# Half tiles of w_out, two top-k blocks side by side, and an earlier S5 and GLU in a two-layer hybrid encoder on one core

## What is computed

```python
proj = h @ w_in
q, k, v, qi, ki, wi, u = jnp.split(proj, IN_SPLITS, axis=-1)
attn = dsa_attention(q, k, v, qi, ki, wi)      # 128 best keys of each query by an index score
y = s5_ssm(u, ...)                             # diagonal state space scan over 512 channels
y = jax.nn.gelu(y)
y = y * jax.nn.sigmoid(y @ glu_w + glu_b)
mixed = jnp.concatenate([rms_norm(attn, attn_gain), rms_norm(y, ssm_gain)], axis=-1)
return mixed @ w_out                           # (512, 1024) @ (1024, 1024)
```

## Time and profile before

| | |
|---|---|
| median of 3 runs | 2172.32 us (2168.12 to 2175.24) |
| time of the profiled execution | 2174.77 us |
| its span | 2172.8 us |
| PE busy, share of the span | 2066.5 us, 95% |
| DVE busy | 1347.1 us, 62% |
| ACT busy | 706.7 us, 33% |
| mean granted clock of TensorE | 0.951 |

### The profile page before, as it was taken

How to read it: one execution, slowest core, us unless ns; L and a number is a source line. 1 busy time by engine, 2 the same in 40 slices (tenths; PEclk the granted TensorE clock), 3 DMA queues, 4 the chain that set the end, 5 groups by cost and what they waited for, 6 DMA issues and landing times.

```text
span 2172.8 us, 25378 instructions
## 1 busy us (share of the span) xinstructions
PE 2066.5 (95%) x9564; PEld 1666.1 (77%) x9564; DVE 1347.1 (62%) x2099; ACT 706.7 (33%) x1066; POOL 243.1 (11%) x219
## 2 busy tenths in 40 slices
PE   6999899999689999999999999999978999999998
PEld 5788778877467788888888877888755678888887
DVE  5768846567884664543467787466688646555334
ACT  3332222342434432222342322234234433222123
POOL 0006900300000000000000294040000000000000
PEclk8999999999669999999999999999986799999999
DMA  7475556342110263533347364553330024454332
GB/s 261 126 214 179 161 147 179 97 113 69 49 39 11 87 202 118 187 97 104 88 125 223 119 196 131 156 146 101 88 88 20 20 59 158 143 165 128 114 90 75
DMA packets 395985, 264.77 MB, mean 122 GB/s; under 512 B 56560, under 2 KB 371672, under 8 KB 395864
## 3 DMA queue, kind: packets, MB, share of 16 engines
q1 hardware_dynamic: 386784, 259.89, 40.1%
q10 hardware_dynamic: 9080, 3.26, 0.7%
HBM read 254.98 MB, written 6.29 MB: 120 GB/s over the span
## 4 chain that ended last, share of the span: by engine, by line
PE 76%; DVE 14%; issue 5%; ACT 3%; DMA 1%; ACTq 0%; SPq 0%; DVEq 0%; POOL 0%; POOLq 0%
PE ps L1650 22%; PE ps L1651 22%; PE ps L1652 22%; DVE w_lo L990 3%; DVE mod_acc L1011 2%; DVE score L1367 2%; DVE small L1365 2%; PE ps L1910 1%; PE ps L1929 1%; ACT w_hi L684 1%; PE ps L1937 1%; PE ps L1920 1%; DVE x L1096 1%; DMA stage<-in_ffn_w 1%; PE ps L1858 1%
## 5 line engine op out<-in xcount | busy, mean ns | idle before, releaser
L1650 PE MATMUL ps<-h_hi,w_hi 128*128 128x512 f32 x1728 | 687.4, 398 | 17.7 <-DVE w_lo L990 13.8
L1651 PE MATMUL ps<-h_lo,w_hi 128*128 128x512 f32 x1728 | 679.4, 393 | 0.0
L1652 PE MATMUL ps<-h_hi,w_lo 128*128 128x512 f32 x1728 | 679.1, 393 | 0.0
L990 DVE TENSOR_TENSOR w_lo<-stage,w_hi 128x1024 fp32r<-128x1024 f32 (+2 forms) x322 | 394.4, 1248 | 103.2 <-ACT w_hi L684 99.3
L1650 PEld LDWEIGHTS ps<-h_hi,w_hi 128*128 128x128 f32 x1728 | 327.5, 190 | 99.0 <-issue 16.4
L1652 PEld LDWEIGHTS ps<-h_hi,w_lo 128*128 128x128 f32 x1728 | 328.1, 190 | 70.0
L1651 PEld LDWEIGHTS ps<-h_lo,w_hi 128*128 128x128 f32 x1728 | 328.0, 190 | 65.7 <-issue 0.5
L684 ACT ACTIVATE w_hi<-stage 128x1024 fp32r<-128x1024 f32 (+2 forms) x322 | 318.7, 1016 | 173.1 <-PE ps L1652 164.9
L1650 PE MATMUL ps<-g_hi,w_hi 128*128 128x512 f32 x704 | 276.4, 393 | 2.4 <-DVE g_lo L1303 2.4
L1651 PE MATMUL ps<-g_lo,w_hi 128*128 128x512 f32 x704 | 274.2, 389 | 0.0
L1652 PE MATMUL ps<-g_hi,w_lo 128*128 128x512 f32 x704 | 274.1, 389 | 0.0
(11 more groups left out here) (300 smaller groups left out, 1859.1 us busy)
## 6 DMA issues: line engine op xcount, KB each, us to landing
stage<-in_ffn_w SPq DMA_DIRECT2D x210, 512.0 KB, 4.6
mod_stage<-in_mod_w SPq DMA_DIRECT2D x144, 512.0 KB, 5.5
stage<-in_ffn_w SPq DMA_DIRECT2D x64, 448.0 KB, 4.0
stage<-in_w_in SPq DMA_DIRECT2D x20, 512.0 KB, 4.0
...
```

Of the source, the lines that this page charges most:

```text
L990: V.tensor_tensor(w_lo[:, c % RING, 0:n], stage[:, c % RING, 0:n], w_hi[:, c % RING, 0:n].bitcast(F32), ALU.subtract).then_inc(w_split_lo. ...
L1650: mm(out, hi, rhs_hi, start=first, stop=False)
L1651: mm(out, hi, rhs_lo, start=False, stop=False)
L1652: return mm(out, lo, rhs_hi, start=False, stop=last)
```

## The change

- w_out is loaded in half tiles. Chunks 16 to 19 of the mixer hold the y half for two output tiles each, chunks 20 to 23 the attention half. The bytes are the same.
- The y halves of output tiles 0 to 3 (y_half) run inside heads 19 to 22, and their part is added to x on its own in heads 20 to 23 (mix_update). Those tiles get a second update later, so four more DVE instructions stand in a layer. keep_streaming begins at head 24.
- Behind head 31 PE runs the y halves of tiles 4 to 7, then eight attention halves (att_half) on their own. Splits 20 and 21 move into heads 21 to 24, splits 22 and 23 ahead of the updates; two of the eight steps still have a split.
- Top-k: a round is topk_max and topk_take, each waiting for its own block's last step (mark, need) and with its own eight values. Two blocks run side by side: 1 and 2 in heads 0 to 7, 2 and 3 in heads 8 to 15, 3 alone in heads 16 to 23, one round a block and head. Eight rounds of block 1 run before head 0, four of them between the index scores.
- S5: states after tiles 4, 5, 6 and 8, outputs after 5, 6, 7 and 9, with three buffers u8 in place of two, and SP's stores and fetches for them move with it. All four GELUs are computed ahead of head 0. The GLU is one group of 12 matmuls in each of heads 4 to 7, and what follows it (norm, ssm_t, mix_done) ends in head 18, not 27.

```diff
 FFN_CHUNKS = 2 * FT + KT * NP
-X_STEPS = 2 * NP * KT + KT
-X_LAST = ((NP - 1) * KT, NP * KT, NP * KT + KT + (NP - 1) * KT)
+EARLY_OUT = 4
+MIX_STEPS = EARLY_OUT + KT
+X_STEPS = 2 * NP * KT + MIX_STEPS
+X_LAST = ((NP - 1) * KT, NP * KT + EARLY_OUT, NP * KT + MIX_STEPS + (NP - 1) * KT)
...
-STATES_AT = {5: 0, 6: 1, 9: 2, 10: 3}
-Y_AT = {7: 0, 8: 1, 10: 2, 11: 3}
+STATES_AT = {4: 0, 5: 1, 6: 2, 8: 3}
+Y_AT = {5: 0, 6: 1, 7: 2, 9: 3}
...
-GLU_AT = {8 + 2 * n + j: (n, j) for n in range(ST) for j in range(2)}
...
+GLU_AT = {4 + n: n for n in range(ST)}
...
+HALF_AT = {19 + n: n for n in range(EARLY_OUT)}
+HALF_X_AT = {20 + n: n for n in range(EARLY_OUT)}
...
-KEEP_FROM = 22
...
-OUT_SPLIT_AT = {10: 16, 12: 17, 15: 18, 17: 19}
+KEEP_FROM = 24
+TOPK_WITH = [(1, 2)] * HEADS + [(2, 3)] * HEADS + [(3,)] * HEADS + [()] * HEADS
...
+    def mark(self, i):
+
+        i.then_inc(self.sem, 1)
+        self.n += 1
+        return self.base + self.n
+
+    def need(self, value):
+
+        self.eng.wait_ge(self.sem, value)
+
...
+                if m < 20:
+                    return tiles(a["w_out"], layer, AT, ST, (m - 16) * 2 * P, 2 * P)
+                return tiles(a["w_out"], layer, 0, AT, (m - 20) * 2 * P, 2 * P)
 
...
-                            if m == 9:
-                                u_store(l, 0)
-                                u_store(l, 1)
-                                u_fetch(l, 0)
-                                u_fetch(l, 1)
-                            if m == 10:
-                                u_store(l, 2)
-                                u_store(l, 3)
-                            if m in (14, 15):
-                                y_store(l, m - 14)
-                                u_fetch(l, m - 12)
-                                y_fetch(l, m - 14)
-                            if m in (17, 18):
-                                y_store(l, m - 15)
-                                y_fetch(l, m - 15)
+                            if 8 <= m < 12:
+                                u_store(l, m - 8)
+                            if 9 <= m < 12:
+                                u_fetch(l, m - 9)
+                            if m in (12, 13, 14, 16):
+                                y = min(m - 12, ST - 1)
...
-                    step(V.memset(score[b][0:64, (b + 1) * P - 64:(b + 1) * P], INADM))
-
-                def topk_round(b):
-
-                    s = score[b]
+                    dve.wait_ge(*idx_acc.at(l, b * IDX_HEADS - 1))
+                    topk_last[b] = step.mark(V.memset(score[b][0:64, (b + 1) * P - 64:(b + 1) * P], INADM))
+
+                def topk_max(b):
+
+                    step.need(topk_last[b])
                     settle(dve)
-                    step(V.max(top8[:], s))
+                    topk_last[b] = step.mark(V.max(top8[b % 2], score[b]))
+
+                def topk_take(b):
+
+                    step.need(topk_last[b])
                     settle(dve)
-                    step(V.match_replace(out=s, in_to_replace=top8[:], in_values=s, imm_value=TAKEN))
+                    topk_last[b] = step.mark(V.match_replace(out=score[b], in_to_replace=top8[b % 2], in_values=score[b], imm_value=TAKEN))
...
 
+                def mix_update(n, bank, even, c):
+
+                    if n % 2:
+                        used(dve, l, c)
+                    else:
+                        dve.wait_ge(*even.at(l, n // 2))
+                    V.scalar_tensor_tensor(out=x[:, n, :], in0=ps[:, bank, :], scalar=gate[:, 1, n:n + 1],
+                                           in1=x[:, n, :], op0=ALU.mult, op1=ALU.add).then_inc(x_new.sem, 1)
+
...
+                                (topk_max, topk_take)[n % 2](1)
                         topk_start(t - INDEX_FROM + 1)
-                    for _ in range(TOPK_EARLY.get(t, 0)):
...
                     mask_head(e)
+                    if len(blocks) > 1:
+                        topk_max(blocks[1])
+                    if blocks:
+                        topk_take(blocks[0])
                     if b:
                         att_step(b - 1, h)
                     if b > 1 and h == 0:
                         att_step(b - 2, 8)
-                    for _ in range(TOPK_AT.get(e, 0)):
-                        topk_round(TOPK_BLOCK[rounds])
-                        rounds += 1
-                        if rounds == len(TOPK_BLOCK) or TOPK_BLOCK[rounds] != TOPK_BLOCK[rounds - 1]:
-                            topk_end(TOPK_BLOCK[rounds - 1])
+                    if len(blocks) > 1:
+                        topk_take(blocks[1])
...
+                    if e in HALF_X_AT:
+                        n = HALF_X_AT[e]
+                        mix_update(n, 4 + n % 2, half_even, m0 + 16 + n // 2)
...
+                split_lo(l, m0 + 23)
                 for n in range(KT):
-                    if n < KT - 2:
-                        split_lo(l, m0 + 20 + n)
+                    if n in (2, 4):
+                        split_lo(l, m0 + 23 + n // 2)
                     if n:
                         add_squares(l, KT + n - 1)
-                    update(l, 1, n, m0 + 16 + n)
+                    if n >= EARLY_OUT:
+                        mix_update(n, OUT_BANK[n - EARLY_OUT], out_even, m0 + 20 + n // 2)
+                    else:
+                        if n >= 2:
+                            dve.wait_ge(*x_new.at(l, NP * KT + n))
+                        mix_update(n, n % 2, out_even, m0 + 20 + n // 2)
                     scaled_lo(l, 2, n)
...
+                    c = m0 + 16 + n // 2
+                    if n % 2 == 0:
+                        chunk_ready(l, c)
+                    if 2 <= n < 6:
+                        pe.wait_ge(*x_new.at(l, NP * KT + n - 2))
+                    bank = 4 + n % 2 if n < EARLY_OUT else OUT_BANK[n - EARLY_OUT]
+                    for k in range(ST):
+                        if n == 0:
+                            pe.wait_ge(*mix_done.at(l, k))
+                        i = split3(ps[:, bank, :], half_tile(c, k, n % 2), h_hi[:, AT + k, :], h_lo[:, AT + k, :],
+                                   k == 0, n < EARLY_OUT and k == ST - 1)
+                    if n % 2:
                         i.then_inc(w_used.sem, 1)
-
-                def out_half(n, first, last):
-
-                    c = m0 + 16 + n
-                    if first == AT:
+                    elif n < EARLY_OUT:
+                        i.then_inc(half_even.sem, 1)
+
+                def att_half(n):
+
+                    c = m0 + 20 + n // 2
+                    if n % 2 == 0:
                         chunk_ready(l, c)
-                        if n >= 4:
-                            pe.wait_ge(*x_new.at(l, NP * KT + n - 4))
-                    for k in range(first, last):
-                        if n == 0 and k >= AT:
-                            pe.wait_ge(*mix_done.at(l, k - AT))
-                        i = split3(ps[:, OUT_BANK[n % 4], :], w_tile(c, k), h_hi[:, k, :], h_lo[:, k, :], k == AT, k == AT - 1)
-                    if first == 0:
-                        i.then_inc(w_used.sem, 1)
+                    if n in (2, 3):
+                        pe.wait_ge(*x_new.at(l, NP * KT + EARLY_OUT + n - 2))
+                    bank = n % 2 if n < EARLY_OUT else OUT_BANK[n - EARLY_OUT]
+                    for k in range(AT):
+                        i = split3(ps[:, bank, :], half_tile(c, k, n % 2), h_hi[:, k, :], h_lo[:, k, :],
+                                   n < EARLY_OUT and k == 0, k == AT - 1)
+                    i.then_inc((out_even, w_used)[n % 2].sem, 1)
 
...
                     if e in GLU_AT:
-                        glu(*GLU_AT[e])
+                        glu(GLU_AT[e])
+                    if e in HALF_AT:
+                        y_half(HALF_AT[e])
```

More of the change, by code:

```diff
@@ L239, in trunk @@
         small = sb("small", [P, SMALL])
-        ms, rstd, mhalf, cols, top8, rinv, nmax, ones = (small[:, i:i + n] for i, n in (
+        ms, rstd, mhalf, cols, top8a, rinv, nmax, ones = (small[:, i:i + n] for i, n in (
             (0, 4), (4, 4), (8, 4), (12, 4), (16, 8), (24, HEADS), (32, 2), (34, 1)))
+        top8 = (top8a, small[:, 64:72])
         half_bias, half_gain, bias_col = small[:, 54:58], small[:, 58:62], small[:, 62:64]
@@ L922, in mixer_act @@
                 act.wait_ge(*h_done.at(l, 2 * KT - 1))
-                for m in range(2):
-                    act.wait_ge(*y_in[m].at(l, 16 * 2 * GI - 1))
-                    gelu(m)
+                gelu(3)
+                for m in range(ST):
+                    gelu_high(m)
                 for e in range(NA):
@@ L1439, in s5_scan @@
                     half = (slice(0, NS), slice(NS, P))
-                    step(*(V.tensor_tensor(hs[half[g], 0, :, g, 1:J + 1], X[0][half[g]], M[0][half[g]], ALU.subtract) for g in range(2)),
-                         V.tensor_tensor(hs[half[0], 1, :, 0, 1:J + 1], X[1][half[0]], M[1][half[0]], ALU.add))
+                    step.need(re)
```

(17 more changed lines are left out.)

157 lines of the change are left out of this document (92 added, 65 removed).

## The result

The changed kernel takes 2147.19 us (2145.30 to 2147.57), the kernel before, timed beside it, 2171.28. The ratio is 0.9886 [0.9868, 0.9904]: faster by 1.1%, with 2148 forecast. The spans of the two profiled executions differ by 27.0 us.

The account below looks back on a forecast made before the run. PE is busy for 95% of the span, so only waits and slow stretches could go. Terms of -14.3 us (layer 0) and -13.0 (layer 1) from 2174.8 gave 2147.5, so 2148; own range 2138 to 2160, with rivals to 2168.

Parts of the forecast that it names:

- a place that I had set at 0: Start of the next FFN after the mixer: low clock in both kernels, so counted 0, at worst +2 us.
- Ahead of head 0: Before the first logits: scans +0.8 us net, PE's idle wait 4.1 in place of 5.87; sum -1.0 a layer.
- Block 0: Heads 0 to 7: shorter top-k, added GLU, clock rising after 6.4 us; mask 8 at +24.6, sum -0.3 us.
- Block 1: Heads 8 to 15: top-k without gaps and PE work give 31.0 us; -4.4, in layer 1 -3.1.
- the bunching: Block 1: PE's work of about 28 us is bunched in head 13, so 1.5 us was added.
- Block 2: Heads 16 to 23: y_half(0) starts at +11.5, then heads take 2.7 + 1.9 us; mask 24 at +33.5, sum -1.0.
- Block 3: From mask 24 to the last values: PE's head unchanged, one keep_streaming group gone; -0.8 us.
- w_out: End of the mixer: first update 14.1 us behind the last values, not 16.7; steps 25.6, not 29.8; sum -6.8.
- gaps that stay: Rival, top-k rounds: the 0.15 us is a cost of each top-k instruction, not of waiting; 2166 us, chance 0.13.
- a clock that stays low in heads 4 to 7 and 19 to 22: Rival: clock stays at 1.2 GHz through the GLU and y halves; +9 us a layer, 2193 us, chance 0.06.
- costly scans: Rival, early S5: PE's waits between projections bring the clock down; +5 us a layer, 2158 us, chance 0.12.
- half a gain at the end: Rival, w_out: first update stays at 16.7 us and a step waits for ACT; -3, 2156 us, chance 0.08.

Follow-up runs that it names:

- the run with chained waits: The changed kernel, same instruction order, with each top-k step waiting for the last counted DVE step of whichever block, not its own block's: 2154.03 us, 0.9922.

## Why the prediction was right, point by point

- *The sum.* Forecast -14.3 and -13.0 a layer. To the next FFN's first product the trace has -12.9 in layer 0 and -11.3 in layer 1. Another 2.9 us were gained behind layer 1's mixer, a place that I had set at 0. In the kernel before, the first 12 us of the FFN behind the mixer were, in layer 0 (layer 1 has the same, at 0.60):

```profile
733.37:745.37 12.00, 12.00 (x46) 9.74 (x47) 3.68 (x5) 3.03 (x4) 1.98 (x1) 0.61 0.40 116
```

  After, the clock is 0.63 and 0.87 there. PE does wait 6.7 us ahead of both, as forecast (6.5); the low stretch just ends sooner once, and 60 matmuls go into the 12 us instead of 46. I would call that luck; no run isolates it. Without it the sum would have missed by 3 us, still inside the range.
- *Ahead of head 0.* Forecast 4.1 us of idle PE and -1.0; measured 3.45 and -0.7 (layer 1: 3.77). The -0.7 can't be told from nothing, since profiles of kernels that are alike up to there reach mask 0 up to 2.5 us apart; the wait can. A scan takes 6.5, not the 6.7 that I took. The early scans cost PE no more than 0.95 us of wait at one place.
- *Block 0.* 24.6 forecast, 24.75 and 25.9 measured. The clock rose 3.2 us after the first GLU matmul in layer 0 and only behind the twelfth, 5.3 us on, in layer 1; I had taken 6.4. So the block by itself is over a microsecond longer than I forecast, and in layer 0 an early rise hid that: the hit there is luck.
- *Block 1.* 31.0 forecast, 30.1 and 29.4 measured: the bunching that I added didn't cost 1.5. The mechanism was half of the story, though. I took the gap of 0.15 us for the whole gain; the run with chained waits gives it 2.7 and 3.3 us of block 1 in the two layers, of the 5.3 and 4.6 by which the block got shorter.
- *Block 2.* Forecast -1.0, measured -0.1 and, in layer 1, +0.8. This term was mis-sized: y_half(0) starts 13.1 us behind mask 16 and not 11.5, and a head with a y half takes 4.7 to 4.8, not 4.6.
- *Block 3.* -0.8 forecast, -0.4 measured in both layers by the same marks (27.39 and 27.00): the keep_streaming group was worth half of what I took.
- *w_out.* First update 14.2 us behind the last values (14.1 forecast); steps 2.73, 4.75, 3.33, 4.75, 3.33, 3.32, 3.33 (2.7, 4.75, 3.33, 4.75, three of 3.33). -6.2 in place of -6.8.

The rivals: gaps that stay, a clock that stays low in heads 4 to 7 and 19 to 22, costly scans and half a gain at the end are each refuted by the trace. The Trainium skill, "VectorE: DVE Perf Modes", section "The DRAIN you can't avoid", has it that a semaphore after each DVE instruction costs nothing over one at the end, by a measurement on copies. Here, for steps that wait for the one just ahead, it cost 0.15 us each, and 7 us in all. The price that I had put on the rival with the gaps was too high, though: with 64 of the 96 gaps ahead of a value load back, the run with chained waits lost 3.4 us a layer, where I had put 9.5 on all of them.

What the prediction did not see is that its own terms hide parts of very different worth. By the runs, from the kernel before on: top-k order -25 us beside its own runs of the kernel before (2146), early S5 and GELUs -7 (2139), early GLU +17 (2156), half tiles and y halves -9 (2147). The single runs of the kernel at 2156 lie 9 us apart, so the last two are rough each; their sum, between 2139 and 2147, is not. They belong together, since the y halves need the GLU's result by head 19, and together they cost 8 us. A table of windows before and after could not show this, because the loss of one part and the gain of another fell in the same block.

Open is whether early GLU would pay for itself in a version with skewed steps against one without it: the skewed steps need half tiles, and no kernel here has those with a late GLU.
